# First span's convolution groups between its attention items, sample chunk first in the query stage

## What is computed

```
b_g, c_g, x_in, q_lat, kv_lat, kr_raw, gate_c, gate_a = in_projection(rmsnorm(x), w_in)
u      = c_g * x_in;  conv_y = conv3_causal(u)          # per channel, 3 taps
qn     = rmsnorm(q[..., :64]);  qr = rope(rmsnorm(q[..., 64:]))   # per head, from q_lat
kn     = rmsnorm(ckv @ w_uk)                            # per head
attn   = softmax(mask(qn @ kn.T + qr @ kr.T)) @ ckv @ w_uv
x      = x + (sigmoid(gate_c) * ((b_g * conv_y) @ w_conv_out)
              + sigmoid(gate_a) * (attn @ w_attn_out)) @ w_mix_out
x      = x + peer(rmsnorm(x))                           # 8 heads x 16 experts of 16384, gathered rows
```

## Time and profile before

| | |
|---|---|
| median of three runs | 3627.61 us |
| the profiled execution, device time | 3623.42 us |
| its span, first to last instruction | 3621.5 us |
| query stage, about | 157.5 to 292.0 us |
| span 0: attention with its output transposes | 292.0 to 363.5 us |
| span 0: channel groups | 363.5 to 407.7 us |
| span 0: gates to mixing | 407.7 to 520 us |
| first gather | 559.6 us |
| PE, DVE, ACT, POOL busy over the span | 84%, 70%, 37%, 30% |

### The profile page before, as it was taken

The page is one execution under the profiler, slowest core; times in us unless marked ns, Lnnn a source line. Parts: engine busy times, 40 slices in busy tenths (PEclk is TensorE's granted clock), DMA queues, the critical chain, the costliest instruction groups (busy, mean ns, idle before and its releaser), DMA issues.

```text
span 3621.5 us, 33491 instructions
## 1 busy us (share of the span) xinstructions
PE 3045.7 (84%) x9652; PEld 1697.9 (47%) x9652; DVE 2549.4 (70%) x5686; ACT 1347.1 (37%) x3945; POOL 1095.1 (30%) x1252
## 2 busy tenths in 40 slices
PE   7986998778899999577778898899688988878877
PEld 4534885334555555233434454445245545455421
DVE  3232127987677789977677867789987787756864
ACT  2223013368422233356553222343344444423343
POOL 0000003333333334333333333333333333333342
PEclk9985999788999999788989998899898998866999
DMA  3111448999999999899999999999999999989998
GB/s 122 51 40 50 154 132 360 406 389 395 380 419 423 391 366 360 328 411 398 395 416 420 422 420 422 407 422 400 411 392 415 390 417 402 374 352 416 422 421 366
DMA packets 235102, 1274.62 MB, mean 352 GB/s; under 512 B 45198, under 2 KB 65486, under 8 KB 99366
## 3 DMA queue, kind: packets, MB, share of 16 engines
q0 software_dynamic: 152064, 1107.36, 74.9%
q1 hardware_dynamic: 81126, 160.72, 12.5%
q10 hardware_dynamic: 1728, 4.39, 0.3%
HBM read 1258.98 MB, written 13.40 MB: 351 GB/s over the span
## 4 chain that ended last, share of the span: by engine, by line
PE 30%; DVE 25%; DMA 22%; issue 7%; ACT 6%; POOL 1%; SPq 0%; DVEq 0%; POOLq 0%; ACTq 0%
DMA tl_uv<-in_uv,tl_idx 22%; DVE tl_uv L1507 9%; PE tl_y L924 9%; PE tl_f L1179 7%; DVE tl_acc L1488 5%; PE tl_f L1207 2%; PE tl_f L1154 2%; PE tl_f L1190 2%; PE tl_f L1098 1%; PE tl_f L985 1%; PE tl_f L1049 1%; POOL tl_uv L855 1%; PE tl_f L1121 1%; DVE tl_eq L1607 1%; ACT L1254 1%
## 5 line engine op out<-in xcount | busy, mean ns | idle before, releaser
L855 POOL DMA_INDIRECT tl_uv<-in_uv,tl_idx x1056 | 1048.4, 993 | 1884.9 <-PE tl_y L924 1121.5
L1507 DVE CUSTOM_DVE_ANT_0 tl_uv<-tl_uv,tl_h 128x1024 f32<-128x1024 f32 x1056 | 1266.9, 1216 | 405.4 <-DMA tl_uv<-in_uv,tl_idx 390.9
L924 PE MATMUL tl_y<-tl_uv,tl_diag 128*128 128x512 f32 (+1 forms) x2460 | 1290.9, 666 | 294.4 <-ACT tl_diag L1226 275.1
L924 PEld LDWEIGHTS tl_y<-tl_uv,tl_diag 128*128 128x128 f32 (+1 forms) x2460 | 481.6, 207 | 952.4 <-issue 499.4
L1254 ACT ACTIVATE tl_ge<-tl_a 128x1 f32<-128x1 f32 x1056 | 210.4, 199 | 1244.1 <-DVE tl_a L1507 1205.5
L1488 DVE SCALAR_TENSOR_TENSOR tl_acc<-tl_uv,tl_w,tl_acc 128x1024 f32<-128x1024 f32 x433 | 554.9, 1282 | 80.8 <-ACT tl_w L1238 78.2
L1238 ACT ACTIVATE tl_w<-tl_ge,tl_weight 128x1 f32<-128x1 f32 x1024 | 301.7, 295 | 33.3
L1207 PE MATMUL tl_f<-H,w_tail 128*128 128x384 f32 (+2 forms) x1024 | 264.1, 413 | 8.6 <-DVE H L1820 7.3
L1226 ACT ACTIVATE tl_diag<-K,tl_w 128x128 f32<-128x128 f32 (+1 forms) x615 | 244.4, 397 | 48.2 <-PE tl_y L924 29.0
L1179 PE MATMUL tl_f<-H,w_tail 128*128 128x256 f32 (+2 forms) x768 | 234.0, 461 | 2.1 <-DVE tl_ya L1788 2.1
L1207 PEld LDWEIGHTS tl_f<-H,w_tail 128*128 128x128 f32 x1024 | 180.8, 196 | 103.8 <-issue 37.1
(11 more groups left out here) (233 smaller groups left out, 2912.5 us busy)
## 6 DMA issues: line engine op xcount, KB each, us to landing
w_tail<-in_w_merge SPq DMA_DIRECT2D x80, 512.0 KB
w_tail<-in_w_peer SPq DMA_DIRECT2D x64, 576.0 KB
w_tail<-in_w_conv SPq DMA_DIRECT2D x36, 512.0 KB
tl_uv<-in_uv,tl_idx POOLq DMA_INDIRECT x1056
w_tail<-in_w_mix SPq DMA_DIRECT2D x32, 512.0 KB
X<-in_cache SPq DMA_DIRECT2D x48, 128.0 KB
X<-in_x SPq DMA_DIRECT2D x8, 536.0 KB, 7.1
o_y<-tl_acc ACTq DMA_DIRECT2D x8, 512.0 KB
```

Source lines behind the costliest of these rows:

```text
L855: pool.indirect_dma_start(UV[:, u % RING, :], None, d["uv"], bass.IndirectOffsetOnAxis(ap=which, axis=0)).then_inc(landed[u % RING], 16)
L924: mm = pe.matmul(Y[0:m, half * 512:(half + 1) * 512], DG[:, (pe_count[u] - 1) % DIAGS, 0:m], UV[:, u % RING, D + half * 512:D + (half + 1) ...
L1507: dve.tensor_tensor_reduce(UV[:, u % RING, 0:D], UV[:, u % RING, 0:D], HP[:], 1.0, 0.0, ALU.mult, ALU.add, A[:, t % 2, i:i + 1]).then_inc( ...
```

## The change

Query stage: the chunks are taken in the order `ASKED`, the one with the sample tokens first. Their copying out and `asked` follow the first chunk's rotation, and the products with the key weights stand in two halves, before the third chunk's projections and before their block 5, in one PSUM bank. Keys, queries and rotated queries are stored separately, each when it is done. SP starts the first three `w_tail` loads at the stage's beginning.

Tail stage, span 0: keys, values, probabilities, scores and queries lie in the memory of `UV`. Channel group 0 stands ahead of the attention, group x+1 after the scores of item x; the twelve are through at step 10. ACT's and DVE's part of a group stands at the same place of their order. These groups use the four PSUM banks that PEER's tensors have later. SP's weight loads 3 to 14 stand between the loads of the heads. Other spans are as before.

```
+ASKED = [CHUNKS[2], CHUNKS[0], CHUNKS[1]]
...
+            for w in range(WRING):
+                following.start(sp, w)
-            for c, (a, n) in enumerate(CHUNKS):
+            for c, (a, n) in enumerate(ASKED):
                 s, lo, hi = c % 2, max(a, META), min(a + n, KEYS)
+                sp.wait_ge(normed, at(c, 4))
+                sp.dma_start(d["s_k"]..., RAW[:, s, 0:4, 0:hi - a]).then_inc(k_stored[s], 16)
+                sp.wait_ge(normed, at(c, 8))
+                sp.dma_start(d["s_qn"]..., RAW[:, s, 4:8, lo - a:hi - a]).then_inc(qn_stored[s], 16)
                 sp.wait_ge(ready, c + 1)
...
+            def absorbed(b):
+                pe.wait_ge(asked, 1)
...
+                if c == NC - 1:
+                    absorbed(0)
                 for j in range(NJ):
+                    if c == NC - 1 and j == 5:
+                        absorbed(1)
...
                     if j == 0 and c >= 2:
-                        act.wait_ge(stored[s], 48 * (c // 2))
+                        act.wait_ge(asked, 1)
+                        act.wait_ge(k_stored[s], 16 * (c // 2))
+                    if j == 4 and c >= 2:
+                        act.wait_ge(qn_stored[s], 16 * (c // 2))
...
+        keys_room = lambda c: flat if c else rows_flat          # rows_flat is UV
+        beside = lambda c, x: [x + 1] if c == 0 and x + 1 < NCV else []
...
                 for h in range(2, NH):
+                    if c == 0:
+                        for w in (2 * h - 1, 2 * h):
+                            sp.wait_ge(proj, last_use(w - WRING))
+                            weights.start(sp, w)
                     qk(h)
                     if h > 2:
                         values(h - 1)
                 values(NH - 1)
-                sp.wait_ge(proj, ready[c, AVAL, len(items[c]) - 1])
+                if c:
+                    sp.wait_ge(proj, ready[c, AVAL, len(items[c]) - 1])
...
             def attention(c, a):
                 n = len(items[c])
+                if c == 0:
+                    channel(c, 0, a)
                 for x in range(n + 4):
...
                     if x < n:
                         att_score(c, x, a)
+                    for g in beside(c, x):
+                        channel(c, g, a)
```

More of the change, by code:

```diff
@@ L624, in tail_stage @@
                         order += [asc(c, x, g) for g in range(sgroups(items[c][x][1]))]
+                    order += [(c, CHAN, g) for g in beside(c, x)]
                 order += [(c, AOUT, t) for t in range(len(PARTS[c]))]
@@ L646, in tail_stage @@
         for g, (c, kind, i) in enumerate(order):
-            if kind >= ASCORE:
+            if kind == CHAN and c == 0:
+                bank = 4 + i % 4
+            elif kind >= ASCORE:
                 bank = next(quartet)
@@ L1120, in att_value, with channel @@
                     m = P if j < i + 1 else META
-                    mm = pe.matmul(F[:, bank_of[c, AVAL, x], 0:VH], AP[0:m, x % 2, j, :], att_v(s)[0:m, j, :],
+                    mm = pe.matmul(F[:, bank_of[c, AVAL, x], 0:VH], probs(c, x)[0:m, j, :], att_v(c, s)[0:m, j, :],
                                    start=(j == 0), stop=(j == i + 1))
+                mm.then_inc(proj, 1)
+            def channel(c, g, a):
+                halo = 2 if c == 0 else 0
+                s = arrived(c * GROUPS + g)
+                bank_free(c, CHAN, g)
+                for k in range(KD):
+                    mm = pe.matmul(F[:, bank_of[c, CHAN, g], 0:halo + wide(c)], W[:, s, k, :],
+                                   H[:, k, META + a - halo:META + a + wide(c)], start=(k == 0), stop=(k == KD - 1))
                 mm.then_inc(proj, 1)
@@ L1147, in _ @@
                     decode()
[L1148 to L1149 removed]
+                for g in range(lead(c) if c else 0):
                     units(due(c, g - NCV, 0))
[L1151 to L1156 removed]
+                    channel(c, g, a)
                 for ob in range(KD):
@@ L1383, in attention @@
                         att_power(c, x - 2)
+                    for g in beside(c, x):
+                        if g % 3 == 0:
+                            channel_gate(c, g // 3)
                 units(due(c, -1 - NCV, LAG_ACT))
@@ L1738, in attention @@
+            def attention(c, n):
+                if c == 0:
+                    dve.wait_ge(conv_in, 32)
+                for x in range(len(items[c]) + 3):
                     units(due(c, x - PRE[c], LAG_DVE))
-                    if x < n:
+                    if x < len(items[c]):
                         att_maxima(c, x)
```

267 lines of the change are left out of this document (149 added, 118 removed).

## The result

| | before | after |
|---|---|---|
| median of the runs | 3627.68 us (4 runs) | 3593.89 us (3590.14 to 3596.45, 4 runs) |
| ratio, with its 95% interval | | 0.9903 [0.9886, 0.992] |
| span of the profiled execution | 3621.5 us | 3588.3 us |
| PE's first matmul of the query stage to the tail's first DMA | 134.4 | 132.8 |
| tail's first DMA to the gates' first matmul | 115.7 | 84.9 |

The kernel is faster by 33.8 us, where 43.5 was forecast; 3593.9 lies inside the range of 3577 to 3598. The four stretches account for the profiled pair: 1.6 + 30.8 - 2.9 + 2.7 us, and 1.0 that the stage ahead of the query stage happened to be shorter, make 33.2 = 3621.5 - 3588.3. Of these, 1.0 and 2.7 us come from stretches that the change leaves alone.

The account below looks back on a forecast made before the run. POOL's gathers, 3061.5 us at DMA share 0.99, bound the kernel, so an earlier start moves the end. Savings 5.1 + 21.9 + 11.1 + 1.8 + 0.3 + 3.3 = 43.5 us gave 3584.1 us, range 3579 to 3589, with rivals 3577 to 3598.

Parts of the forecast that it names:

- rival A: Clock falls behind the last channel group, attention steps 11 to 19 stay at 28.6 us: 14.3 lost, 3598 us; chance 0.18.
- Rival C: The gather stretch takes back a third of the gain, 14 us: 3598 us; chance 0.06.
- Steps 1 to 3: Tail: first loads' wait saves 5.1 us, channel groups' 44.2 only move, attention steps 0 to 10 save 21.9.
- Step 4: Attention steps 11 to 19, without groups: 17.5 us for 28.6 if the clock stays up, 11.1 saved.
- Step 5: End of the attention: PE's work halves and a weight wait goes, 3.7 us becomes 1.9, 1.8 saved.
- Step 6: Weight loads 3 to 14 on SP, between the heads' loads: slack some 0.7 us each, cost taken 0.
- rival B: Weights come late to the channel groups: 4 to 5 us lost, 3589 us; chance 0.10.
- Step 7: Query stage's stall: 9.5 us becomes 6 and work from elsewhere; 0.3 us saved, between -1 and +1.5.
- Step 8: Query stage's end: products gone, tail's first DMA at 288.7 instead of 292.0; 3.3 us saved, up to 1.5 more.
- Everything from the gates to the end is the same program and moves up by that: Gates to kernel end: unchanged program, starts earlier by the summed 43.5 us.
- Rival D: Clock never rises while channel groups and attention are interleaved: slower, 3651 us; chance 0.03.

Follow-up runs that it names:

- the second round: The changed kernel, unaltered, measured again in another profiled execution: 3595.61 us against 3622.62 for the kernel before, ratio 0.9919.
- e4: The changed kernel plus four superfluous 32-column matmuls behind the scores in each of steps 11 to 18; ratio to the kernel before 0.9932.
- e3: The changed kernel plus one superfluous 512-column matmul behind the scores in each of steps 11 to 18; ratio to the kernel before 0.99.
- e5: The changed kernel with channel groups cut into halves, spread over attention steps 0 to 18; 3574.69 us against 3626.37 before, ratio 0.9852.
- e6: The changed kernel with all products in one piece ahead of the third chunk, even and odd heads in turn, two PSUM banks; ratio to before 0.9895.
- e1: The changed tail with the old query stage order and the three early weight loads; 3586.82 us against 3621.22 for the kernel before, ratio 0.9899.

## Why the prediction was right, and where it was wrong

Right in kind: the tail is the gain, 30.8 of 33.2 us, and what moves the first gather's start moves the end, within the scatter. But 3593.9 is outside the forecast's own range of 3579 to 3589. It lies inside 3577 to 3598 because that range was stretched for the rivals A and C, and 3.7 of the 33.2 us (1.0 ahead of the query stage, 2.7 in the gathers) were luck; the 27.0 us of the second round would give 3600.7, outside it.

- *Steps 1 to 3* (first loads, groups, attention steps 0 to 10): forecast 27.0, measured 27.1. The clock rose 5.4 us into the gapless work, not 4.5.
- *Step 4* is the one that failed: "At 2.4 GHz the work halves and the idle stays ... if the clock stays up." It did not; rival A, given 0.18, happened. 2.3 us saved instead of 11.1. (The busy share of that sum, 11.2 of 17.5 us, is 64%, and not the 60 or 61% that the prediction writes.) The reason for the wrong choice: I took a stretch of span 1 in which the clock held for a statement on waits ("no single wait reaches 1.65 us"). There, in the kernel before, the clock fell only at about 767.6, 1.8 us after that wait had ended and in the middle of small matmuls. And the work between the waits was not the same. PE also ran wide matmuls there, which steps 11 to 19 of span 0 lack:

```profile
752.85 1.98 PE L924 MATMUL tl_y<-tl_uv,tl_diag 128*128 128x512 f32 x4 [0.94 <-ACT tl_diag L1226]
...
767.00:768.00 1.00, 1.00 (x8) 0.82 (x6) 0.95 (x2) 0.93 (x4) 0.49 (x1) 0.78 1.06 442
```

In the experiments e4 shows that PE without waits loses the clock too, while e3 and e5 keep it. The rule of the Trainium skill on micro-idles (TensorE: Matmul & The Clock Gate, "A second HAM failure mode"), quoted in the prediction, came out right in direction: the clock was low from 349.4 us to behind the gates' start. But it did not swing back in between, and as e4 shows, the idle is not what decides here.
- *Step 5*: 1.4 saved, not 1.8, and the gates lost 1.3 at their low clock where rival A had 2.3.
- *Step 6*: cost 0 was right. PE was never held by a weight load in 56.3 us; rival B fell.
- *Step 7*: the stall came as described (PE started its products 63.5 us into the stage, forecast 63.7). The term for the products was mis-sized: 3.62 + 1.97 us, not 1.8 + 0.9. "Half of 3.64" assumed that a product's price does not depend on its neighbours or its bank (e6). And 1.6 us of low clock behind the second half was not in the sum. The third chunk's rotation ended 3.8 us later in the stage than before, where 0.3 earlier was forecast.
- *Step 8*: 5.4 saved, not 3.3. From the last rotation to the tail's first DMA 3.8 us instead of 9.2: the stores landed in half the time. The prediction named that as "up to 1.5 more"; it was 2.1.
- *"Everything from the gates to the end is the same program and moves up by that"*: 2.9 us were lost up to the first gather, nearly all of it clock and over half of it no doing of the change, and 2.7 gained behind it, which is within the scatter. Rival C did not happen at its size: the kernel after's two stretches, 3059.2 and 3069.9, stand on either side of the one of the kernel before, 3061.9, and no kernel's is longer than that by more than 9.8 us. A smaller loss is not excluded.
- *Rival D* fell at once: the clock rose in the interleaved stretch.

Together: 43.5 - 9.1 (steps 1 to 5) - 2.0 (7 and 8) - 2.9 (gates to gather) + 1.0 (ahead of the query stage) + 2.7 (gathers) = 33.2 us.

## What to carry to other kernels

Where one engine waits a little in every step of a loop, spread independent wide work thinly over all steps rather than thickly over the first ones: here twelve groups in eleven steps saved 31 us up to the gates, the same groups cut in half over nineteen steps 46. Before halving a stage's time because the clock will be high, look at what PE executes there and not only at how long it waits, and price both outcomes. When a batch of small matmuls is split, check which rows of the array and which PSUM bank neighbours use: here the split doubled the price of each. And before a few microseconds are put down to a change, look at the same place in other executions: at four places here a clock that goes either way made 1 to 4 us.

## What the hardware showed that was not expected

- PE next to gapless can lose the high clock: in e4 it fell at about 351.5 us behind a single wait of 0.17 us and stayed at 0.50 with PE busy 5.00 of 5.00 us; in the kernel after it fell behind sixteen records of 64x32 products with no gap at all (3.50 of 3.50 us at 0.57). One matmul of 512 columns, or four of 258, in each step kept it at 1.00 with the same small matmuls around them.
- The same wait with the same work around it leaves the clock up in one execution and down in another. Behind the 3.5 us wait before PEER it was up in two of thirteen executions and down in eleven; behind the 2.8 us wait at the query stage's start up in eleven and down in two (e1, e4); behind the second half of the products, without a wait, down in six of seven. What else decides stays open.
- Matmuls of 64 rows, at 1.2 GHz: 32 records in 3.64 us when the halves of the array and two PSUM banks take turns, 16 in 3.62 us with one half and one bank.
- Stores of 320 to 360 KB on SP's queue landed in 5.1 to 5.4 us when the other stores of the chunk were issued in front of them, in 2.3 to 2.5 when those had gone out earlier.
